# Expert matmuls of a hybrid encoder step: one 32-bit product for a high/low split, and six weight buffers for three

## The chip, the cores and the metric

One core of a Trainium2 chip. The metric is the device time of one execution in microseconds (us), the median of several runs. The kernel before takes 1567.64 us (three runs, 1567.49 to 1568.17).

## What is computed

One layer of a streaming encoder on 288 rows (256 prompt rows and 32 sample rows), width 2048, all in float32: a projection `h @ w_in` to 8704 columns, stick-breaking and sliding-window attention, two output projections merged under sigmoid gates, `w_out`, and then the part that the change touches, a mixture of 16 gated experts of which each row uses two:

```python
def hier_moe(h, ...):
    ...
    for e in range(N_EXPERTS):
        a = jax.nn.silu(hf @ w_e_gate[e]) * (hf @ w_e_up[e])
        y = y + gate[:, e:e + 1] * (a @ w_e_down[e])
```

`w_e_gate` and `w_e_up` are 16 x 2048 x 512, `w_e_down` is 16 x 512 x 2048: 12 MB of weights for each expert, 192 MB in all.

## The kernel before, in words

Everything up to the experts is not rewritten by the change: the projections work through `w_in`, `w_sb_o`, `w_swa_o` and `w_out` in blocks of 128 columns. ScalarE copies a block into `wh` (type F32R, L590), VectorE puts the rest into `wl` (L1206), and TensorE makes three products for each of 16 contraction tiles (`products`, L865 to L867). A queue of SyncE loads the blocks as pairs into `ring`; the last four iterations (IT_OUT to IT_END) load `w_out`. `load` then fetches the three matrices of expert 0 into `slot_g` (gate), `slot_d` (down) and `slot_u` (up), 4 MB each. GpSimd meanwhile brings `xT` back from memory for the residual sum.

Then `choose` (VectorE) compares row ranks with 0 to 63 and so makes `pick`, a matrix of 0 and 1 that picks the rows of one expert, 64 slots. `gather` (TensorE, L1064) multiplies `pick` with the rows `x2` (three bf16 parts, three row tiles: nine matmuls for each of 16 tiles of 128 columns, 144 in all) and so leaves the expert's rows, transposed, in banks 0 and 1. `slot_rms` (L1072) gathers the row scales, and `gathered` (L1479) multiplies by the norm's weight into `hg`, 128 x 16 x 64.

The expert's matmuls run in F32R. `hgx` holds beside each other the F32R copy of `hg` (64 columns, L767) and what it leaves out (64 columns, L1487). Each of 24 pieces of an expert's weights (128 x 1024) is copied by ScalarE into `eh` (`high`, L760), and VectorE, or GpSimd for pieces 1, 9 and 18, puts the rest into `el` (`low_part`, L340). TensorE makes two matmuls with `eh` and two with `el`, all with `hgx` as the stationary operand, whose 128 columns fill all 128 partitions of the result bank (`up_gate_piece`, L1090). Partitions 0 to 63 and 64 to 127 are then added up (L781, L1564 for the gate, L789, L1567 for up), ScalarE applies silu (L785), VectorE multiplies (L1570). Four matmuls turn the product (L1110), it is split again into `aTx` (L792, L1578), and pieces 16 to 23 multiply with it into banks 4 to 7 (L1120). ScalarE copies the upper halves into `y_sb` (L806), VectorE adds the lower ones (L1591), and SyncE writes the rows (L434).

The order of the work is written out by hand. TensorE's queue gathers the rows of the next expert one tile behind each piece from the fourth piece on, the last three tiles behind the sixteenth. SyncE waits until the last piece of a matrix is split (`low_wait`) and then loads the same matrix of the next expert (`next_matrices`).

```python
sem, w = piece(c)
act.wait_ge(S[sem], s * 16 + 16 * (1 + c // CH))
act.wait_ge(S["ch_used"], used(s, c - AHEAD - 1))
a_.activation(eh[c % 4][:], w, ACT.Copy).then_inc(S["eh_ready"], 1)
...
for low, part in enumerate((eh[c % 4], el[c % 4])):
    for k in range(2):
        kt = c % 8 * 2 + k
        mm = mm_(ps[2 + c // 8][:], hgx[:, kt, :], part[:, k * DE:(k + 1) * DE],
                 start=(low == 0 and kt == 0), stop=(low == 1 and kt == KT - 1))
```

Of the kernel before, what the change touches and what calls it, by code (L numbers as in the profile page):

```python
# [30 lines left out]
F32 = mybir.dt.float32  # L31
F32R = mybir.dt.float32r
# [7 lines left out]
P = 128  # L40
# [26 lines left out]
PIECE = D // 2  # L67
CH = 24
BY_POOL = (1, 9, 18)
AHEAD = 3  # L70
# [22 lines left out]
def constants():  # L93
# [27 lines left out]
    for t, n in enumerate(TILES):  # L121
# [6 lines left out]
RAISED = """z_sb o_sb h_turned pool_head m_done a_ready y_out nat_done zm_done e_done o_sb_ev nat_free  # L128
            rope_done ml_done y_act y_dve aT_ps aTl_done table_in ev_a ev_d""".split()
# [31 lines left out]
def build(nc, x_prompt, x_sample, cache_sb_k, cache_sb_v, cache_swa_k, cache_swa_v, w_in, b_gate, swa_sink,  # L161
# [66 lines left out]
    slot_g = at("slot_g", 100, [P, KT, DE])  # L228
    slot_u = at("slot_u", 132, [P, KT, DE])
    slot_d = at("slot_d", 0, [P, FT, D])  # L230

    places = (164, 168, 172, 176, 180, 184, 188, 60)
    eh = [at(f"eh{j}", places[2 * j], [P, PIECE], F32R) for j in range(AHEAD + 1)]
    el = [at(f"el{j}", places[2 * j + 1], [P, PIECE], F32R) for j in range(AHEAD + 1)]

# [4 lines left out]
    hgx = at("hgx", 32, [P, KT, 2 * SLOTS], F32R)  # L240
    hg = at("hg", 40, [P, KT, SLOTS])
    aTx = at("aTx", 44, [P, FT, 2 * SLOTS], F32R)
    pick = at("pick", 46, [P, 3, SLOTS], BF16)
    y_sb = at("y_sb", 50, [SLOTS, D])
    g_sb = at("g_sb", 58, [SLOTS, DE])
    u_sb = at("u_sb", 201, [SLOTS, DE])
# [12 lines left out]
    gfin = at("gfin", 156, [P, D])  # L259
# [41 lines left out]
    with ExitStack() as ctx:  # L301
# [7 lines left out]
                   g_in u_in d_in picked hg_ps hg_sb hgh_done hgl_done eh_ready el_ready elp_ready ch_used g_low g_sum  # L309
                   silu_done u_low u_sum a_ready aT_ps aTh_done aTl_done y_act y_dve y_out  # L310
                   zero_set zero_out rows_ready ints_ready gf_in y_in0 y_in1 y_in2 sum_done fin out_done
                   ex_in ex_out half_done ssq3 rko_done ident_done rp_done x2_back all_rows table_in""".split()
# [16 lines left out]
        def piece(c):  # L329

            m, q = c % CH // 8, c % 8
            if m == 2:
                return "d_in", slot_d[:, q // 2, q % 2 * PIECE:(q % 2 + 1) * PIECE]
            w = (slot_g, slot_u)[m]
            return ("g_in", "u_in")[m], w[:, 2 * q:2 * q + 2, :].rearrange("p k n -> p (k n)")

        def low_part(eng, s, c):

            eng.wait_ge(S["eh_ready"], s * CH + (c + 1))
            (nc.gpsimd if eng.engine == mybir.EngineType.Pool else nc.vector).tensor_tensor(  # L340
                el[c % 4][:], piece(c)[1], eh[c % 4][:].bitcast(F32), ALU.subtract)\
                .then_inc(S["elp_ready" if c % CH in BY_POOL else "el_ready"], 1)

        def used(s, c):


            return s * CH + (c + 2 + AHEAD)

# [21 lines left out]
        def _(sp):  # L370
# [28 lines left out]
            with sp.Fori(IT_OUT, IT_END) as it:  # L399
# [4 lines left out]
            def load(dst, w, e, sem):  # L404
                sp.dma_start(dst[:], w[0, ds(e, 1)].rearrange("a (k p) n -> p (a k) n", p=P)).then_inc(S[sem], 16)

            sp.wait_ge(S["blk"], upto(IT_OUT - 1, 3))
            load(slot_g, w_e_gate, 0, "g_in")  # L410
            sp.wait_ge(S["wl_ready"], upto(IT_END - 1, 3))
            load(slot_d, w_e_down, 0, "d_in")
            sp.wait_ge(S["x2_d"], 12)
            load(slot_u, w_e_up, 0, "u_in")

            def low_wait(s, c):


                assert not any(c - AHEAD <= p <= c for p in BY_POOL)
                sp.wait_ge(S["el_ready"], s * (CH - len(BY_POOL)) + (c + 1 - sum(p <= c for p in BY_POOL)))  # L420
# [1241 lines left out]
```

## Time and profile before

| | |
|---|---|
| median of three runs | 1567.64 us |
| the profiled execution: span from first to last instruction | 1563.4 us |
| median less the span | 4.2 us |
| mean granted TensorE clock | 0.914 of 2.4 GHz |
| PE busy, DVE busy, ACT busy, POOL busy | 87%, 63%, 54%, 12% |
| read and written | 319.51 MB, 20.71 MB |
| first expert matmul, last expert matmul | 826.0 us, 1513.8 us |

The profiled execution's own time is its span and what lies around it; of that the profile shows the span, and the median of the runs lies 4.2 us above it. PE is TensorE's matmuls, PEld its loads of the stationary operand, DVE VectorE, ACT ScalarE, POOL GpSimd, SPq the queue of SyncE. A matmul in plain float32 appears as two records, one in F32R as one.

### The profile page before, as it was taken

The page shows a single profiled execution, that of the slowest core. Times are in us where ns is not written, and L with a number is a line of the kernel's source. Part 1 is how long each engine was busy: PE and PEld are TensorE (multiplying, and loading weights), DVE is VectorE, ACT ScalarE, POOL GpSimd, SP SyncE. Part 2 cuts the span into 40 slices and gives each one's busy share as a digit, 9 for nine tenths or more (in the row PEclk, how much of TensorE's full clock was granted, in tenths as well). Part 3 has the DMA queues.
Part 4 walks back from the last instruction along what each step waited for, and adds up shares of the span by engine and source line. Part 5 has one row for each costly group of instructions (what it writes and reads, how often), then busy time and mean ns, then how long its engine had stood idle before and what let it go on. Part 6 is the DMA issues. An engine that isn't in the chain of part 4 may idle for free.

```text
span 1563.4 us, 24761 instructions
## 1 busy us (share of the span) xinstructions
PE 1365.0 (87%) x9452; PEld 1151.7 (74%) x9452; DVE 978.9 (63%) x1156; ACT 846.1 (54%) x993; POOL 184.6 (12%) x154
## 2 busy tenths in 40 slices
PE   5989999799999999999968888888898889888861
PEld 3889999698889999989946666666666566666630
DVE  3524446434445545444547887778877887888876
ACT  3423232355555454532446777667766777677741
POOL 2100100111100000000001111111111111111111
PEclk9899999899999999999978998889988898889985
DMA  7664444413334444464635887878877887877805
GB/s 234 227 225 163 173 161 162 169 55 107 107 108 161 162 161 161 161 222 161 244 133 216 309 299 291 302 281 311 313 274 302 335 305 287 307 285 294 320 15 208
DMA packets 184097, 340.48 MB, mean 218 GB/s; under 512 B 2944, under 2 KB 105456, under 8 KB 173184
## 3 DMA queue, kind: packets, MB, share of 16 engines
q1 hardware_dynamic: 179760, 319.30, 56.5%
q0 software_dynamic: 3904, 17.22, 3.2%
q10 hardware_dynamic: 400, 3.51, 0.6%
q8 instruction: 22, 0.36, 0.1%
q14 instruction: 11, 0.09, 0.0%
HBM read 319.51 MB, written 20.71 MB: 218 GB/s over the span
## 4 chain that ended last, share of the span: by engine, by line
PE 54%; issue 22%; DVE 12%; ACT 8%; DMA 4%; DVEq 1%; ACTq 0%; POOL 0%; POOLq 0%; SPq 0%
PE bank L1090 16%; PE bank L865 8%; PE bank L867 7%; PE bank L866 7%; PE bank L1120 5%; PE bank L1064 5%; ACT eh L760 3%; DVE el L340 2%; DVE y_sb L1591 2%; PE bank L1110 1%; DMA ring<-in_w_in 1%; DVE g_sb L1570 1%; ACT wh L590 1%; PE bank L843 1%; DVE wl L1206 1%
## 5 line engine op out<-in xcount | busy, mean ns | idle before, releaser
L1206 DVE TENSOR_TENSOR wl<-ring,wh 128x2048 fp32r<-128x2048 f32 x100 | 229.2, 2293 | 214.7 <-ACT wh L590 214.6
L865 PE MATMUL bank<-xh,wh 128*128 128x288 f32 x1088 | 331.3, 305 | 10.9 <-DVE xl L1214 5.9
L866 PE MATMUL bank<-xl,wh 128*128 128x288 f32 x1088 | 324.0, 298 | 0.0
L867 PE MATMUL bank<-xh,wl 128*128 128x288 f32 x1088 | 323.2, 297 | 0.0
L590 ACT ACTIVATE wh<-ring 128x2048 fp32r<-128x2048 f32 x100 | 190.9, 1909 | 145.8 <-PE bank L867 133.7
L1090 PE MATMUL bank<-eh,hgx 128*128 128x512 f32 x512 | 200.1, 474 | 62.6 <-DVE el L340 42.2
L865 PEld LDWEIGHTS bank<-xh,wh 128*128 128x128 f32 x1088 | 206.7, 190 | 15.7 <-issue 8.7
L867 PEld LDWEIGHTS bank<-xh,wl 128*128 128x128 f32 x1088 | 207.9, 191 | 0.0
L866 PEld LDWEIGHTS bank<-xl,wh 128*128 128x128 f32 x1088 | 207.6, 191 | 0.3
L340 DVE TENSOR_TENSOR el<-slot_u,eh 128x1024 fp32r<-128x1024 f32 x112 | 143.9, 1305 | 50.4 <-ACT eh L760 50.2
L760 ACT ACTIVATE eh<-slot_d 128x1024 fp32r<-128x1024 f32 x128 | 133.7, 1055 | 68.8 <-PE bank L1120 48.2
L1090 PE MATMUL bank<-el,hgx 128*128 128x512 f32 x512 | 169.1, 412 | 0.0
L760 ACT ACTIVATE eh<-slot_u 128x1024 fp32r<-128x1024 f32 x128 | 134.2, 1055 | 56.3 <-PE bank L1090 56.1
L340 DVE TENSOR_TENSOR el<-slot_g,eh 128x1024 fp32r<-128x1024 f32 x112 | 157.7, 1447 | 5.6 <-ACT eh L760 5.5
L1064 PEld LDWEIGHTS bank<-pick,x 128*128 128x128 bf16 (+1 forms) x2304 | 100.9, 100 | 80.2 <-issue 57.9
L340 DVE TENSOR_TENSOR el<-slot_d,eh 128x1024 fp32r<-128x1024 f32 x112 | 135.4, 1223 | 38.3 <-ACT eh L760 38.0
L1090 PEld LDWEIGHTS bank<-eh,hgx 128*128 128x128 f32 x512 | 81.8, 200 | 100.9 <-DVE el L340 62.7
L1064 PE MATMUL bank<-pick,x 128*128 128x64 bf16 (+1 forms) x2304 | 143.2, 201 | 4.0 <-DVE pick L1472 4.0
L760 ACT ACTIVATE eh<-slot_g 128x1024 fp32r<-128x1024 f32 x128 | 126.2, 1044 | 17.8 <-PE bank L1090 17.8
L1090 PEld LDWEIGHTS bank<-el,hgx 128*128 128x128 f32 x512 | 103.2, 202 | 25.9
L1120 PE MATMUL bank<-eh,aTx 128*128 128x512 f32 x256 | 104.5, 497 | 19.0 <-DVE aTx L1578 19.0
L1120 PE MATMUL bank<-el,aTx 128*128 128x512 f32 x256 | 96.3, 463 | 0.0
(303 smaller groups left out, 1936.2 us busy)
## 6 DMA issues: line engine op xcount, KB each, us to landing
ring<-in_w_in SPq DMA_DIRECT2D x34, 2048.0 KB, 8.1
slot_g<-in_w_e_gate SPq DMA_DIRECT2D x16, 4096.0 KB, 13.2
slot_d<-in_w_e_down SPq DMA_DIRECT2D x16, 4096.0 KB, 12.9
slot_u<-in_w_e_up SPq DMA_DIRECT2D x16, 4096.0 KB, 13.3
ring<-in_w_out SPq DMA_DIRECT2D x8, 2048.0 KB, 7.6
ring<-in_w_sb_o SPq DMA_DIRECT2D x8, 1024.0 KB, 5.0
ring<-in_w_swa_o SPq DMA_DIRECT2D x8, 1024.0 KB, 7.2
y_rows<-y_sb SPq DMA_DIRECT2D x16, 512.0 KB, 7.2
```

The costliest lines, as they stand in the source:

```text
L340: (nc.gpsimd if eng.engine == mybir.EngineType.Pool else nc.vector).tensor_tensor(el[c % 4][:], piece(c)[1], eh[c % 4][:].bitcast(F32), AL ...
L590: a_.activation(wh[:, j % 2], raw(j), ACT.Copy).then_inc(S["wh_ready"], 1)
L760: a_.activation(eh[c % 4][:], w, ACT.Copy).then_inc(S["eh_ready"], 1)
L843: mm = tr(ps[2 + k % 3][:, t * P:t * P + n], x_nat[0:n, t, k * P:(k + 1) * P], ident[0:n, 0:n])
L865: mm_(dst, wh[:, j % 2, k, :], hi[:, k, :], start=(k == k0), stop=False)
L866: mm_(dst, wh[:, j % 2, k, :], lo[:, k, :], start=False, stop=False)
L867: mm = mm_(dst, wl[:, j % 2, k, :], hi[:, k, :], start=False, stop=(k == k1 - 1))
L1064: mm_(ps[k // 8][:, (k % 8) * SLOTS:(k % 8 + 1) * SLOTS], x2[j][0:n, t, k * P:(k + 1) * P], pick[0:n, t, :], start=(t == 0 and j == 0), st ...
L1090: mm = mm_(ps[2 + c // 8][:], hgx[:, kt, :], part[:, k * DE:(k + 1) * DE], start=(low == 0 and kt == 0), stop=(low == 1 and kt == KT - 1))
L1120: mm = mm_(ps[4 + q0 + q][:], aTx[:, f, :], part[:, q * 512:(q + 1) * 512], start=(low == 0 and f == 0), stop=(low == 1 and f == FT - 1))
L1206: v.tensor_tensor(wl[:, j % 2], raw(j), wh[:, j % 2].bitcast(F32), ALU.subtract)\
L1591: v.tensor_tensor(y, y, ps[4 + q][0:SLOTS, :], ALU.add).then_inc(S["y_dve"], 1)
```

## The change

For the experts alone, the split is taken out: the weights as they are loaded, float32, are the moving operand, `hg` (float32, 64 columns) is the stationary one, and the result fills partitions 0 to 63 of a bank; gate and up take turns tile by tile in banks 2 and 3. The three slots of 32 KB per partition become six homes of 16 KB: homes 0 to 3 hold four tiles of gate and four of up each, homes 4 and 5 half of down each. An expert's matrices are laid out so that partition p holds rows 16p to 16p+15 of gate and up (4p to 4p+3 of down): a home's load reads runs of 8 KB (gate, up) and 16 KB (down), where the loads before read 2 KB and 8 KB. So that the rows fit, `gather` and the turn read their stationary operand with a step: every 16th column of `x2`, every fourth of `g_sb`. SyncE loads a home again as soon as its matmuls are through. The gathering for the next expert stands in two pieces behind all of gate and up.

```diff
+    home = [at(f"home{c}", kb, [P, 4096]) for c, kb in enumerate((100, 116, 138, 154, 0, 16))]
...
+        def gate_up(half, k):
+            return home[k // KPC][:, half * 2048 + k % KPC * DE:half * 2048 + (k % KPC + 1) * DE]
+        def down(f, q):
+            return home[GU + f // 2][:, f % 2 * D + q * 512:f % 2 * D + (q + 1) * 512]
...
+            def load_home(c, e):
+                if c < GU:
+                    for half, w in enumerate((w_e_gate, w_e_up)):
+                        src = w[0, ds(e, 1)].rearrange("a (p k) n -> p (a k) n", p=P)[:, c * KPC:(c + 1) * KPC, :]
+                        sp.dma_start(home[c][:, half * 2048:(half + 1) * 2048].rearrange("p (k n) -> p k n", n=DE), src)\
+                            .then_inc(S[f"home_in{c}"], 16)
+                else:
+                    f = 2 * (c - GU)
+                    src = w_e_down[0, ds(e, 1)].rearrange("a (p f) n -> p (a f) n", p=P)[:, f:f + 2, :]
+                    sp.dma_start(home[c][:].rearrange("p (f n) -> p f n", n=D), src).then_inc(S[f"home_in{c}"], 16)
...
             def next_matrices(e, s):
-                low_wait(s - 1, 7)
-                load(slot_g, w_e_gate, e, "g_in")
-                low_wait(s - 1, 15)
-                load(slot_u, w_e_up, e, "u_in")
-                low_wait(s - 1, 23)
-                load(slot_d, w_e_down, e, "d_in")
+                for c in range(HOMES):
+                    sp.wait_ge(S["ch_used"], s * HOMES + (c + 1 - HOMES))
+                    load_home(c, e)
...
+                act.wait_ge(S["ch_used"], s * HOMES + GU)
+                a_.activation(g_sb[:], ps[2][0:SLOTS, :], ACT.Silu, scale=stat[0:SLOTS, 24:25])\
+                    .then_inc(S["silu_done"], 1)
                 act.wait_ge(S["aT_ps"], s + 1)
+                a_.activation(aT[:], ps[4][:, 0:FT * SLOTS].rearrange("p (f n) -> p f n", f=FT), ACT.Copy)\
+                    .then_inc(S["aT_sb"], 1)
...
+                for k in range(k0, k1):
+                    for t, n in enumerate(TILES):
+                        for j in range(3):
+                            mm_(ps[k // 8][:, (k % 8) * SLOTS:(k % 8 + 1) * SLOTS],
+                                x2[j][0:n, t, k:D:KT], pick[0:n, t, :],
...
             def expert(s, nxt):
+                pe.wait_ge(S["hg_sb"], s * 2 + 2)
+                for k in range(KT):
+                    c = k // KPC
+                    if k % KPC == 0:
+                        pe.wait_ge(S[f"home_in{c}"], s * 32 + 32)
+                    for half in range(2):
+                        mm = mm_(ps[2 + half][0:SLOTS, :], hg[:, k, :], gate_up(half, k),
+                                 start=(k == 0), stop=(k == KT - 1))
+                    if k % KPC == KPC - 1:
+                        mm.then_inc(S["ch_used"], 1)
                 if nxt:
+                    gather(s + 1, 0, 12)
+                pe.wait_ge(S["a_ready"], s + 1)
                 for f in range(FT):
-                    mm = mm_(ps[2][:, f * SLOTS:(f + 1) * SLOTS], g_sb[:, f * P:(f + 1) * P],
+                    mm = mm_(ps[4][:, f * SLOTS:(f + 1) * SLOTS], g_sb[:, f:DE:FT],
                              ident[0:SLOTS, 0:SLOTS], start=True, stop=True)
                 mm.then_inc(S["aT_ps"], 1)
+                if nxt:
+                    gather(s + 1, 12, KT)
+                    pe.wait_ge(S["y_dve"], s + 1)
+                    slot_rms()
+                pe.wait_ge(S["aT_sb"], s + 1)
+                if nxt:
+                    pe.wait_ge(S["hg_sb"], s * 2 + 4)
...
+                for f in range(FT):
+                    if f % 2 == 0:
+                        pe.wait_ge(S[f"home_in{GU + f // 2}"], s * 16 + 16)
+                    for q in range(4):
+                        mm = mm_(ps[4 + q][0:SLOTS, :], aT[:, f, :], down(f, q),
+                                 start=(f == 0), stop=(f == FT - 1))
```

How the order moves on TensorE's queue, in the body of the loop over the experts. Before, a piece and the gathering behind it stand so (`eh_108` and `el_112` are the fourth buffers of the two parts, `x_0` to `x_2` the three bf16 parts of `x2`; a row is one instruction, or several of the same with x):

```order
L1082 REGISTER_ALU
L1090 MATMUL bank<-eh_108,hgx 128x512 [waits el_ready]
L1090 MATMUL bank<-eh_108,hgx 128x512
L1090 MATMUL bank<-el_112,hgx 128x512 x2
L1064 MATMUL bank<-pick,x_0_113 128x64
L1064 MATMUL bank<-pick,x_1_114 128x64
L1064 MATMUL bank<-pick,x_2_115 128x64
```

Each piece waits for its own `el`. In the changed kernel the loop begins with all of gate and up (`home_102` to `home_105` are homes 0 to 3), and the gathering stands behind it:

```order
+L1009 ISA [waits hg_sb]
+L1011 MATMUL bank<-home_102,hg 64x512 [waits home_in0]
+L1011 MATMUL bank<-home_102,hg 64x512 x7
+L1011 MATMUL bank<-home_103,hg 64x512 [waits home_in1]
+L1011 MATMUL bank<-home_103,hg 64x512 x7
+L1011 MATMUL bank<-home_104,hg 64x512 [waits home_in2]
+L1011 MATMUL bank<-home_104,hg 64x512 x7
+L1011 MATMUL bank<-home_105,hg 64x512 [waits home_in3]
+L1011 MATMUL bank<-home_105,hg 64x512 x7
+L987 ISA
+L991 MATMUL bank<-pick,x_0_108 128x64 [waits picked]
```

Thirty-two matmuls for gate and up stand where 64 stood, and none of them waits for another engine's work on the weights. The end of the same body, from the last rows of the gathering to the down matmuls:

```order
+L991 MATMUL bank<-pick,x_2_110 128x64
+L999 MATMUL bank<-rparts,pick 64x1 [waits y_dve]
+L999 MATMUL bank<-rparts,pick 64x1 x8
+L1028 REGISTER_ALU [waits aT_sb]
+L1033 ISA [waits y_dve,y_act,hg_sb]
+L1035 MATMUL bank<-home_106,aT 64x512 [waits home_in4]
+L1035 MATMUL bank<-home_106,aT 64x512 x7
+L1035 MATMUL bank<-home_107,aT 64x512 [waits home_in5]
+L1035 MATMUL bank<-home_107,aT 64x512 x7
```

Sixteen matmuls stand for 32, and ahead of them a wait that was not there: for `hg_sb`, the rows of the next expert. On SyncE's queue, homes 0 and 1 of expert 0 now stand between two pairs of `w_out`:

```order
+L356 DMA ring<-in_w_out 128x16x256 [waits wl_ready] x2
+L384 DMA home_102<-in_w_e_gate 128x2048 [waits blk]
+L384 DMA home_102<-in_w_e_up 128x2048
+L384 DMA home_103<-in_w_e_gate 128x2048
+L384 DMA home_103<-in_w_e_up 128x2048
```

Before, the first expert load stood behind all of the `w_out` loads.

## Rows read from the trace of the kernel before

**Rows 1.** The page, chain that ended last: shares of the span by engine

```profile
PE 54%; issue 22%; DVE 12%; ACT 8%; DMA 4%; DVEq 1%; ACTq 0%; POOL 0%; POOLq 0%; SPq 0%
```

**Rows 2.** Stretch, its us, busy PE, PEld, DVE, ACT, POOL; clock, DMA share, GB/s

```profile
826.00:1472.50 646.50, 570.38 (x3856) 404.40 (x3856) 523.75 (x536) 459.11 (x520) 111.43 (x45) 0.88 0.80 297
```

**Rows 3.** Waits of PE in the expert stage: us in total, times, longest

```profile
PE bank L1090 <- DVE el L340: 42.2, 16, 2.8
PE bank L1120 <- DVE aTx L1578: 19.0, 16, 2.4
```

**Rows 4.** Timeline of PE, one expert: start us, us, what, count, idle before

```profile
1013.53 0.54 PE L1064 MATMUL bank<-pick,x 128*128 128x64 bf16 x9
1013.99 0.73 PE L1090 MATMUL bank<-eh,hgx 128*128 128x512 f32 x2
1014.57 0.63 PE L1090 MATMUL bank<-el,hgx 128*128 128x512 f32 x2
1015.03 0.54 PE L1064 MATMUL bank<-pick,x 128*128 128x64 bf16 x9
...
1024.07 1.95 PE L1064 MATMUL bank<-pick,x 128*128 128x64 bf16 x36
1025.95 0.53 PE L1072 MATMUL bank<-rparts,pick 128*64 128x1 bf16 x9
1026.85 1.81 PE L1110 MATMUL bank<-con,g_sb 64*128 64x64 f32 x8 [0.37 <-DVE g_sb L1570]
1029.77 1.22 PE L1120 MATMUL bank<-eh,aTx 128*128 128x512 f32 x2 [1.10 <-DVE aTx L1578]
1030.78 1.05 PE L1120 MATMUL bank<-el,aTx 128*128 128x512 f32 x2
```

**Rows 5.** Timeline of PE, the plain float32 logits (288 columns moving)

```profile
787.90 5.03 PE L1021 MATMUL bank<-xT,wr 128*20 128x288 f32 x20
792.86 1.53 PE L1016 MATMUL bank<-con,xT 128*128 128x128 f32 x12
```

**Rows 6.** Timeline of PE, a plain float32 matmul of 448 columns in attention

```profile
322.30 0.91 PE L966 MATMUL bank<-spb,con 128*128 128x448 f32 x2
323.05 0.38 PE L967 MATMUL bank<-spb,con 128*128 128x128 f32 x2
```

**Rows 7.** Timeline of all engines, from the first gathering to the first expert matmul

```profile
810.33 11.25 PE L1064 MATMUL bank<-pick,x 128*128 128x64 bf16 x144 [3.95 <-DVE pick L1472]
...
821.50 0.73 PE L1072 MATMUL bank<-rparts,pick 128*64 128x1 bf16 x9
822.27 1.29 DVE L1479 TENSOR_TENSOR hg<-bank,par 128x512 f32<-128x512 f32 x2 [11.41 <-PE bank L1072]
...
826.04 1.22 PE L1090 MATMUL bank<-eh,hgx 128*128 128x512 f32 x2 [3.81 <-DVE hgx L1487]
```

**Rows 8.** Timeline of PE, first and last matmuls of the last expert

```profile
1472.49 0.70 PE L1090 MATMUL bank<-eh,hgx 128*128 128x512 f32 x2
...
1513.15 0.63 PE L1120 MATMUL bank<-el,aTx 128*128 128x512 f32 x2
```

**Rows 9.** The chain that ended last, behind the last expert

```profile
1517.64 4.31 DMA y_rows<-y_sb
```

**Rows 10.** Timeline of DVE at the first residual sums of w_out

```profile
688.26 0.45 DVE L1364 TENSOR_TENSOR xT<-xT,bank 128x288 f32 x1 [8.07 <-DMA xT<-xT_spill]
```

**Rows 11.** DMA issues of the page: KB each, us to landing

```profile
slot_g<-in_w_e_gate SPq DMA_DIRECT2D x16, 4096.0 KB, 13.2
```

**Rows 12.** Two stretches of PE: its us, busy us; clock, DMA share, GB/s

```profile
815.00:820.00 5.00, 5.00 (x67) 0.50 0.01 3
1024.10:1026.90 2.80, 2.43 (x47) 1.00 0.99 364
```

**Rows 13.** Groups of PEld: loads of the stationary operand, busy us and mean ns

```profile
L1090 PEld LDWEIGHTS bank<-eh,hgx 128*128 128x128 f32 x512 | 81.8, 200 | 100.9 <-DVE el L340 62.7 <-POOL el L340 23.4 <-issue 4.3
L1064 PEld LDWEIGHTS bank<-pick,x 128*128 128x128 bf16 x1536 | 64.1, 103 | 65.6 <-issue 57.9 <-DVE rk L1467 4.0
```

More of the change, by code:

```diff
@@ L66 @@
 PAIR = 2 * P
[L67 to L70, printed above, removed]
+HOMES = 6
+GU = 4
+KPC = KT // GU
 FAR = 1000.0
@@ L239, in build @@
     lgT = at("lgT", 58, [NL, NT])
-    hgx = at("hgx", 32, [P, KT, 2 * SLOTS], F32R)
-    hg = at("hg", 40, [P, KT, SLOTS])
-    aTx = at("aTx", 44, [P, FT, 2 * SLOTS], F32R)
+    hg = at("hg", 32, [P, KT, SLOTS])
+    aT = at("aT", 36, [P, FT, SLOTS])
+    y_sb = at("y_sb", 38, [SLOTS, D])
+    g_sb = at("g_sb", 58, [SLOTS, DE])
+    gf_pk = at("gf_pk", 205.90625, [P, KT])
     pick = at("pick", 46, [P, 3, SLOTS], BF16)
-    y_sb = at("y_sb", 50, [SLOTS, D])
-    g_sb = at("g_sb", 58, [SLOTS, DE])
-    u_sb = at("u_sb", 201, [SLOTS, DE])
     su_b = at("su_b", 206, [P, P], BF16)
@@ L398, in _ @@
                         .then_inc(S["w_load1"], 16)
-            with sp.Fori(IT_OUT, IT_END) as it:
+            def load_home(c, e):
[8 more added lines that the diff above has]
+                    sp.dma_start(home[c][:].rearrange("p (f n) -> p f n", n=D), src).then_inc(S[f"home_in{c}"], 16)
+            for j in range(2):
+                slot_free(j, IT_OUT)
+                load_pair(j, w_out[0, :, j * PAIR:(j + 1) * PAIR])
+            sp.wait_ge(S["blk"], upto(IT_OUT - 1, 3))
+            load_home(0, 0)
+            load_home(1, 0)
+            with sp.Fori(IT_OUT + 1, IT_END) as it:
                 for j in range(2):
@@ L815, in _ @@
+            with act.Fori(0, NE) as e:
+                expert(e)
             act.wait_ge(S["ints_ready"], 1)
@@ L818, in _ @@
                 with act.Fori(0, more) as i:
-                    tokens_high(i + NE)
-                    for c in range(AHEAD):
-                        high(i + NE, c)
-                    expert(i + NE, False)
+                    expert(i + NE)
             for t, n in enumerate(TILES):
@@ L1124, in _ @@
             pe.wait_ge(S["rk_done"], 1)
-            for k in range(KT):
-                gather(0, k)
+            gather(0, 0, KT)
             pe.wait_ge(S["rp_done"], 1)
@@ L1135, in _ @@
                 with pe.Fori(0, more) as i:
-                    for k in range(KT):
-                        gather(i + NE, k)
-                    pe.wait_ge(S["aTl_done"], i + (NE + 1))
+                    gather(i + NE, 0, KT)
                     slot_rms()
@@ L1453, in _ @@
             v.tensor_copy(MMb[:], MM).then_inc(S["masks"], 1)
-            def lows(s, *cs):
-                for c in cs:
-                    if c % CH not in BY_POOL:
-                        low_part(dve, s, c)
-            lows(0, 0)
             dve.wait_ge(S["masks"], 1)
```

211 lines of the change are left out of this document (36 added, 175 removed).

## Prediction

> **What bounds the kernel now.** The chain of waits comes first: TensorE holds 54% of it and "issue" 22%, VectorE and ScalarE 20% together, DMA 4% [rows 1]. The table of stretches says where the change can act: from 826 to 1472.5 us stand fifteen experts, 43.1 us each, with TensorE's matmuls busy 570 of 646.5 us, VectorE 524, ScalarE 459, and the DMA engines 80% at 297 GB/s [rows 2]. The waits in this stage are small: 42.2 us for `el`, 19.0 us for `aTx`, over all sixteen experts [rows 3], some 4 us of the 43 for each. So the stage is TensorE's stream with small holes, and what the change does to that stream decides. The question for the timeline is then what one matmul of each kind costs from start to start. In the steady part of an expert the pair with `el` starts at 1014.57 and its successor at 1015.03: 0.23 us for a matmul of 512 columns; nine gathering matmuls take 0.46 us, 52 ns each [rows 4]. Gate and up are 64 such matmuls, down 32: 22 us of the period. Gathering is 7.5 us.
>
> **The price of a plain float32 matmul** is not in the expert stage, but it is in the trace. The logits move 288 columns of float32 in two records each: 20 records, ten matmuls, from 787.90 to 792.86, so 0.248 us a record, 0.496 us a matmul [rows 5]. In attention one matmul of 448 columns starts at 322.30 and what follows it at 323.05: 0.75 us [rows 6]. Both give 1.67 to 1.72 ns a column; the logits have only 20 stationary columns and the other 128, so the count of stationary columns does not set it, and the 64 of `hg` lie between. For 512 columns I take the longer one's rate, which is the nearer in size: 512 x 0.75 / 448 = 0.857 us (by the logits' rate 0.88). That is 3.7 times an F32R matmul of as many columns, and the change halves their number only: 32 + 16 matmuls, 41.1 us, for 96 that take 22.1.
>
> **The sum, part by part, for one expert at full clock.** (1) Gate and up: 32 x 0.857 = 27.4 us. No `eh` or `el` to wait for; the holes of 4 us go. (2) Gathering, twelve tiles: 108 x 0.052 = 5.6 us. It stands in its own stretch now; before it stood between the pieces, and cost TensorE the same. It covers silu and the product, two operations on 64 partitions, after which the turn can start. (3) The turn: 8 records. At the lower clock they take 1.8 us [rows 4]; I take 1.3. (4) Four more tiles, 1.9 us as in [rows 4], which cover the copy into `aT`. (5) `slot_rms`, then the new wait. Behind the gathering of expert 0, `slot_rms` starts at 821.50, the two products into `hg` at 822.27 and take 1.29 us [rows 7]; with a small copy ahead of them TensorE could go on at 823.8. From that 2.3 us at half clock; 2.1 us here. Queued behind this wait are all down matmuls, and nothing else is there for TensorE. (6) Down: 16 x 0.857 = 13.7 us. (7) The clock. Behind the gathering, `slot_rms` and the small waits of [rows 4] the granted clock falls to 1.2 GHz: the pair at 1029.77 lasts 1.22 us and the next 1.05, where full-clock pairs last 0.63 to 0.73. The new order has the same low stretch ahead of down; some 4 us of down at half clock lose 2.0 us. Sum: 54.0 us, against 43.1.
>
> The last expert has no gathering: 27.4 + about 1.6 for silu and product + 1.6 + 0.6 for turn and copy + 13.7 + 2.0 = 46.9 us. It took 41.3 us, from 1472.49 to 1513.8 [rows 8].
>
> **What lies around it.** The split of the tokens into `hgx` goes, so the first expert starts at 823.8 instead of 826.04 [rows 7]; but the clock is still at its lower level there, and 5 us at the doubled price cost 2.6. Fifteen periods and the last: 823.8 + 2.6 + 15 x 54.0 + 46.9 = 1683.3 us, 169.5 later than 1513.8. Behind it, four copies and four sums of `y_sb` become two copies on each of two engines: rows went out 3.8 us after the last matmul [rows 8, 9], now about 1.5, so -2.3. Homes 0 and 1 are loaded between the `w_out` pairs, while `xT` is still on its way; VectorE waits 8.07 us for it already, until 688.26 [rows 10]. 4 MB take 13.2 us [rows 11]. The bounds are 0 and, if `xT` shares the engines all the way, 4; I take 2. The next pair has some 8 us of slack, so it still comes in time. GpSimd's three pieces and all of `eh` and `el` go at nothing: with the holes of (1) counted, no one waits for them. The sum is 169.2: 1563.4 becomes 1732.6, and with the 4.2 by which the median lies above the span, **1737 us**.
>
> **DMA.** It would have to bring three times 4 MB in a period, 39.6 us at 13.2 us each [rows 11], and there are 54. Homes 0 to 3 come free every 6.9 us of gate and up, the last two in and behind down; each is needed 40 us later. Longer runs only make this looser. It is no bound, and faster loads give nothing.
>
> **The largest unknown** is the step in the gathering's stationary operand, every 16th column of bf16. No row of the trace has such a load. The lower bound is the contiguous load, no extra cost. A gathering matmul takes 52 ns at full clock, and 11.17 us / 144 = 77.6 at half [rows 7, 12]: the 64 moving columns are 27 and 53 ns, so 25 ns are the load's and do not follow the clock. A float32 load of 128 columns lasts 200 ns and the bf16 one 103 [rows 13]; as an upper bound a step could make a bf16 load as slow as that, some 85 to 97 ns more. Between them I take the lower end, as the row of the same operation and size with only the step changed is the nearest. The Trainium skill's page "SBUF — State Buffer" (section "Door 1: The DMA port swizzle") speaks against it: consecutive accesses have full bandwidth within a line of 16 bytes, and each crossing to a new line pays a penalty; here every column crosses. By it the sum would be that of the first rival, and no run here shows it yet.
>
> **Rivals.** *The stepped load costs once more what the contiguous one does*: 77 ns at full clock, 103 at half. TensorE streams less of the time, so the clock falls inside the first gathering run, as it never rises when gathering runs alone [rows 12]. 43 matmuls at 77 ns, 65 at 103: 10.1 us for 5.6, then 3.7 for 1.9, and 0.6 in the small steps; 6.9 a period, 15 times, and 3.7 for expert 0: **1844 us**. The Trainium skill's page named above argues for it. *It costs as much as a float32 load*: 137 and 162 ns, 15.6 a period and 11.8 at the start: 1983. *A float32 matmul into 64 partitions costs half of what the rows say* (the other side): then expert matmuls take 20.6 us, a period some 34 and the loads bound it at 39.6 and rows going out, 41: about **1530 us**. It decides below 0.63 us a matmul, where the period would be 43.1 again. The records at 20 and at 128 stationary columns speak against it, two for each matmul [rows 5, 6]. *Loads come late after all*, since each home waits for its own release and is split in two issues: 5 us a period, 1815. *The clock doesn't rise under float32 at 64 columns*: 82 us of matmuls, about 2350; in [rows 5] it stayed at full through 5 us of such matmuls (0.248 us for 2 x 288 columns is the 2.4 GHz level).
>
> **How the numbers follow.** Forecast 0.53; the doubled load 0.22; as slow as float32 0.10; late loads 0.05; clock 0.02; half the price 0.04; 0.04 for what I don't see, which falls near no change for 0.01. The forecast's own range is 1705 to 1765: 0.02 us on the matmul (0.88 for 0.857) is 1.1 a period and 17 in all, the clock 0 to 4 us a period's half-rate loss, and 2 for `xT`. To hold eight in ten the range must take in the doubled load: 1700 to 1865. Left out are the slow end and the fast one. A measurement of this kernel can tell 0.2%, 3 us, from no change. Faster by more than that 0.04, within it 0.01, slower 0.95.
>
> **What would show it.** Right, if PE's records in the experts start 0.43 us apart at full clock, two a matmul; if the period is 54 us; if home waits are absent from TensorE's waits; and if gathering matmuls stand 52 ns apart. If they stand 77 ns or more apart, the rival with the stepped load holds. If the record count is one a matmul, or the distance is half, the price was wrong and the kernel may be faster. A large wait for a DMA on TensorE would break the paragraph on DMA.

## The result, and the profile after

| | before | the change |
|---|---|---|
| median (range) | 1567.57 us (4 runs) | 1850.47 us (1848.20 to 1851.52, 4 runs) |
| ratio to before, with its 95% interval | 1 | 1.180 (1.1784 to 1.1817) |
| span of the profiled execution | 1563.4 us | 1846.5 us |
| mean granted TensorE clock | 0.914 | 0.902 |
| one expert, start to start | 43.1 us | 61.5 us |

The kernel is 18% slower. The direction was forecast, the size not: 1850 stands 113 us above the 1737 of the forecast and 6 us above the 1844 of the first rival, the stepped load. It is outside the forecast's own range (1705 to 1765) and inside the wide one (1700 to 1865), which had been stretched to take in that rival. The chain that ended last in the profile after answers to [rows 1]; then its costliest groups on TensorE, by line, engine, operands, count, busy us and mean ns:

```profile
PE 84%; DVE 5%; ACT 4%; DMA 3%; issue 3%; ACTq 0%; POOL 0%; DVEq 0%; POOLq 0%; SPq 0%
...
L1011 PE MATMUL bank<-home,hg 128*64 128x512 f32 x1024 | 444.0, 594 | 1.5 <-DVE hg L1387 1.5
...
L1035 PE MATMUL bank<-home,aT 128*64 128x512 f32 x512 | 264.5, 682 | 23.2 <-DVE hg L1387 22.7
```

The records are two a product, as forecast: 512 products of gate and up are 1024 records. VectorE and ScalarE, 20% of the chain in [rows 1], are 9% of it now. That is visible in the stretch of fifteen experts too, whose columns are those of [rows 2]:

```profile
827.70:1750.50 922.80, 900.07 (x3855) 416.79 (x3856) 56.32 (x132) 30.98 (x58) 0.00 (x0) 0.86 0.56 210
```

VectorE fell from 524 us busy to 56 and ScalarE from 459 to 31, the DMA engines from 80% to 56%, and TensorE rose from 570 us to 900. Nearly all that the change took away was work of engines that stood beside the path. What that work had cost TensorE is its idle time, 76 us of the 646.5 in [rows 2]; now it is 23 of 922.8, so some 3.5 us a period were won. The timeline of PE for one expert, beside [rows 4], says what the 61.5 us are (start, us, what, count, idle before):

```profile
1197.61 27.63 PE L1011 MATMUL bank<-home,hg 128*64 128x512 f32 x64
1225.17 9.87 PE L991 MATMUL bank<-pick,x 128*128 128x64 bf16 x108
1234.97 2.12 PE L1019 MATMUL bank<-con,g_sb 64*128 64x64 f32 x8
1237.03 3.43 PE L991 MATMUL bank<-pick,x 128*128 128x64 bf16 x36
1240.38 0.72 PE L999 MATMUL bank<-rparts,pick 128*64 128x1 bf16 x9
1242.62 16.59 PE L1035 MATMUL bank<-home,aT 128*64 128x512 f32 x32 [1.51 <-DVE hg L1387]
```

Gate and up start 27.56 us ahead of the first gathering: 0.861 us a product. The gatherings are what stands out, 9.80 us for 108 (forecast 5.6). Four stretches of this expert, in the columns of [rows 2], show the clock in the first and second part of the first gathering run and of down:

```profile
1225.20:1230.20 5.00, 5.00 (x59) 4.52 (x59) 0.74 (x1) 0.68 (x1) 0.00 (x0) 1.00 0.74 279
1230.90:1234.90 4.00, 4.00 (x45) 3.44 (x45) 0.00 (x0) 0.00 (x0) 0.00 (x0) 0.50 0.23 96
1242.70:1247.30 4.60, 4.60 (x6) 1.36 (x7) 0.00 (x0) 0.00 (x0) 0.00 (x0) 0.50 0.00 0
1247.70:1258.90 11.20, 11.20 (x27) 3.66 (x26) 0.00 (x0) 0.00 (x0) 0.00 (x0) 0.99 0.49 187
```

The clock falls to 1.2 GHz inside the gatherings and stays there for the first 5 us of down. From start to start in the trace a gathering takes 89 ns at full clock and 93 at half, so its price hardly follows the clock. The groups of PEld that answer to [rows 13]:

```profile
L991 PEld LDWEIGHTS bank<-pick,x 128*128 128x128 bf16 x1536 | 116.8, 162 | 27.1 <-issue 12.2 <-DVE rk L1374 1.7
...
L1019 PEld LDWEIGHTS bank<-con,g_sb 64*128 64x128 f32 x128 | 31.0, 324 | 3.3 <-DVE g_sb L1459 2.4
```

The load of the same 128 x 128 bf16 values lasts 162 ns where it lasted 103. TensorE's waits in the expert stage, instead of those of [rows 3], hold no DMA:

```profile
PE bank L1035 <- DVE hg L1387: 22.7, 15, 1.5
PE bank L1019 <- DVE g_sb L1459: 1.6, 1, 1.6
```

### The profile page after: what moved, and what is told of

The parts are those of the page before. It is cut to its first block, busy times and chain, and to the rows that moved or that the text cites. A ratio compares the mean times of both kernels' runs of the same rounds, so it can differ in the third digit from the quotient of the medians.

```text
span 1846.5 us, 22766 instructions
## 1 busy us (share of the span) xinstructions
PE 1716.6 (93%) x9452; PEld 1166.2 (63%) x9452; DVE 475.5 (26%) x724; ACT 389.6 (21%) x500; POOL 62.8 (3%) x107
## 4 chain that ended last, share of the span: by engine, by line
PE 84%; DVE 5%; ACT 4%; DMA 3%; issue 3%; ACTq 0%; POOL 0%; DVEq 0%; POOLq 0%; SPq 0%
PE bank L1011 24%; PE bank L1035 14%; PE bank L991 11%; PE bank L796 10%; PE bank L798 10%; PE bank L797 10%; PE bank L1019 2%; ACT wh L567 1%; DVE hg L1387 1%; DMA ring<-in_w_in 1%; DVE wl L1119 1%; PE bank L774 1%; DMA xT<-xT_spill 1%; DMA yb<-y_rows,rows 1%; DMA con<-in_const 1%
## 5 line engine op out<-in xcount | busy, mean ns | idle before, releaser
L1011 PE MATMUL bank<-home,hg 128*64 128x512 f32 x1024 | 444.0, 594 | 1.5 <-DVE hg L1387 1.5
L1011 PEld LDWEIGHTS bank<-home,hg 128*64 128x64 f32 x1024 | 140.7, 137 | 301.6 <-issue 301.6
L1035 PE MATMUL bank<-home,aT 128*64 128x512 f32 x512 | 264.5, 682 | 23.2 <-DVE hg L1387 22.7
L991 PE MATMUL bank<-pick,x 128*128 128x64 bf16 (+1 forms) x2304 | 213.0, 244 | 1.6 <-DVE pick L1379 1.6
L991 PEld LDWEIGHTS bank<-pick,x 128*128 128x128 bf16 (+1 forms) x2304 | 183.8, 158 | 40.9 <-issue 12.2
L1035 PEld LDWEIGHTS bank<-home,aT 128*64 128x64 f32 x512 | 78.9, 158 | 196.2 <-issue 195.5
L796 PE MATMUL bank<-mh,wh 128*128 128x288 f32 x256 | 77.5, 303 | 6.5 <-DVE wl L1119 3.5
L796 PE MATMUL bank<-oh,wh 128*128 128x288 f32 x256 | 75.9, 297 | 1.8 <-DVE wl L1119 1.8
L797 PE MATMUL bank<-ml,wh 128*128 128x288 f32 x256 | 76.8, 300 | 0.0
L798 PE MATMUL bank<-mh,wl 128*128 128x288 f32 x256 | 76.5, 299 | 0.0
```

The source lines that it names most:

```text
L796: mm_(dst, wh[:, j % 2, k, :], hi[:, k, :], start=(k == k0), stop=False)
L797: mm_(dst, wh[:, j % 2, k, :], lo[:, k, :], start=False, stop=False)
L798: mm = mm_(dst, wl[:, j % 2, k, :], hi[:, k, :], start=False, stop=(k == k1 - 1))
L991: mm_(ps[k // 8][:, (k % 8) * SLOTS:(k % 8 + 1) * SLOTS], x2[j][0:n, t, k:D:KT], pick[0:n, t, :], start=(t == 0 and j == 0), stop=(t == 2 ...
L1011: mm = mm_(ps[2 + half][0:SLOTS, :], hg[:, k, :], gate_up(half, k), start=(k == 0), stop=(k == KT - 1))
L1035: mm = mm_(ps[4 + q][0:SLOTS, :], aT[:, f, :], down(f, q), start=(f == 0), stop=(f == FT - 1))
```

## The experiments

"Period" is the time from the first gate product of expert 0 to that of the last, over fifteen, in the profiled execution. All ratios are to the kernel before, measured beside the run. Averages of a part of an expert are from the start of the part to the start of the next, over fifteen experts.

### Is it the step? Short runs again, nothing stepped

```diff
-    src = w[0, ds(e, 1)].rearrange("a (p k) n -> p (a k) n", p=P)[:, c * KPC:(c + 1) * KPC, :]
+    src = w[0, ds(e, 1)].rearrange("a (k p) n -> p (a k) n", p=P)[:, c * KPC:(c + 1) * KPC, :]
...
-    x2[j][0:n, t, k:D:KT], pick[0:n, t, :],
+    x2[j][0:n, t, k * P:(k + 1) * P], pick[0:n, t, :],
...
-    g_sb[:, f:DE:FT]
+    g_sb[:, f * P:(f + 1) * P]
```

Down's load and the norm weights of `hg` follow.

> The step alone undone, with the runs it bought: feature k*128+p on partition p again for gate and up, feature f*128+p for down, so the gatherings and the turn load adjacent columns and the weights arrive in runs of 2 KB and 8 KB. Unsplit 32-bit products, six homes and their order stay. Theory 1 (the 61.5 us of an expert are 48 full products at 0.858 us, plus 40 ns more for each of 144 gatherings because their stationary operand is stepped by 32 bytes, plus a clock that falls in them): a gathering goes back to 52 ns at full clock (78 at half), the first expert product starts up to 5.9 us earlier (13.4 us to 7.5, or 11.2 at half clock), and a period falls to between 55 and 59 us: 1740 to 1810 us in all, against 1850 with the step. Theory 2 (a gathering is slow because the engine has just done 32-bit work, or because of the clock): it stays near 92 ns and the time within 10 us of 1850. Theory 3 (the long runs carry the transfers): the transfers of an expert grow past 55 us, PE waits for the homes, and the time is above 1850.

Measured: 1755.47 us, ratio 1.117 (1.111 to 1.123), period (1663.78 - 824.81) / 15 = 55.9 us. One expert on PE, then the load's group:

```profile
1162.53 27.63 PE L1011 MATMUL bank<-home,hg 128*64 128x512 f32 x64
1190.09 5.96 PE L991 MATMUL bank<-pick,x 128*128 128x64 bf16 x108
1195.98 1.97 PE L1019 MATMUL bank<-con,g_sb 64*128 64x64 f32 x8
1197.88 2.87 PE L991 MATMUL bank<-pick,x 128*128 128x64 bf16 x36
1200.68 0.72 PE L999 MATMUL bank<-rparts,pick 128*64 128x1 bf16 x9
1202.91 16.87 PE L1035 MATMUL bank<-home,aT 128*64 128x512 f32 x32 [1.51 <-DVE hg L1387]
```

```profile
L991 PEld LDWEIGHTS bank<-pick,x 128*128 128x128 bf16 x1536 | 66.3, 104 | 28.9 <-issue 12.2 <-DVE rk L1374 1.7
```

The gathering is back at 52 ns at full clock and its load at 104. The spans differ by 89 us: 84 are 5.6 us in each of fifteen periods, 2.9 the earlier start of expert 0. No wait for a home appears with runs of 2 KB. Theories 2 and 3 fall. But the clock still falls, and down still takes 16 us.

Where it falls now differs from one expert to the next, with the same instructions. The expert shown is a long one, 57.1 us at a mean clock of 0.88; four of the fifteen take 54.3 to 54.5 at 0.94, and in them the clock stays at full through the turn, which then takes 1.03 us instead of 1.90. The four executions of this kernel spread likewise, from 1739 to 1759 us. In the change the clock fell inside the first gathering run in every one of the fifteen, and the periods behind the first agree within 0.2 us.

### The same with the long runs kept

```diff
-    a_.activation(x2[0][0:n, t, q * 512:(q + 1) * 512], x2_bank(q, t)[0:n], ACT.Copy)
+    a_.activation(packed(x2[0][0:n, t, :], q), strided(x2_bank(q, t)[0:n]), ACT.Copy)
```

`strided` views 512 features as 16 by 32, `packed` puts feature p*16+k at column k*128+p; all pieces, `g_sb` and the residual sum are viewed likewise.

> Long runs kept, both steps undone in another way: the token values are stored so that the columns of one gathering lie side by side (the pieces are written and the residual added back through reordered views), and the gated product is written in the turn's order. Theory 1 (step alone): same period as with short runs, 55 to 59 us; the reordered writes of the token values cost 0 to 10 us once before the experts; 1745 to 1820 us. Theory 2: near 1850. Theory 3 (runs matter): this one is faster than the one with short runs by more than the 10 us of the reordering; under theory 1 it is not.

Measured: 1765.49 us, ratio 1.127 (1.124 to 1.131); period (1664.98 - 824.51) / 15 = 56.0. The same period as with short runs: the long runs bring nothing where TensorE is the bound. The 10 us more are the most that the forecast gave the reordering. The profiled executions are 4 us apart, 1.5 of it in the periods and 2.9 behind the last expert's start, where VectorE adds the residual through reordered views (12 sums, 13.0 us for 8.9).

### How the price grows with the step

```diff
-    x2[j][0:n, t, k:D:KT], pick[0:n, t, :],
+    x2[j][0:n, t, k % 3:k % 3 + STEP[k] * (P - 1) + 1:STEP[k]], pick[0:n, t, :],
```

> The 16 groups of nine gatherings read their 128 columns at steps of 1, 1, 1, 2, 2, 2, 4, 4, 4, 8, 8, 8, 16, 16, 1, 1 columns of 2 bytes: the gathered values are those of wrong columns, and what follows from them too. If the price goes by lines of 16 bytes, steps of 1 take 52 ns at full clock, 2, 4 and 8 grow with the bytes that one column spans, and 16 is no dearer than 8 (92 ns). If any step pays the whole price, 2 already takes 92 ns. If the cost is not the step's, all take 92 ns.

Measured: 1794.96 us in one run, of which only the trace counts here. Stretches of the first gathering run at steps 1, 2, 4 and 8, cut a little inside each, in the columns of [rows 2] with PE alone:

```profile
1205.45:1206.80 1.35, 1.35 (x27) 1.00 0.22 36
1206.90:1208.25 1.35, 1.35 (x28) 1.00 0.80 279
1208.40:1209.90 1.50, 1.50 (x28) 1.00 1.00 421
1210.00:1212.20 2.20, 2.20 (x27) 0.70 0.95 402
```

From start to start in the trace, meaned over fifteen experts: 52.4 ns at step 1, 52.6 at step 2 (4 bytes), 59.2 at step 4 (8 bytes), 87.6 at step 8 (16 bytes) before the clock falls; in the change, at step 16 (32 bytes) and full clock, it is 88.8. At half clock expert 0 gives 78, 78, 80, 94, and 94 at step 16. So the price is reached once each column has 16 bytes to itself, and more step costs hardly more. That is the pattern of the 16-byte line of the Trainium skill's page "SBUF — State Buffer" (section "Door 1: The DMA port swizzle"), which asks for at least two accesses in a line for full bandwidth; at step 4, which has two, the rows show a loss of 7 ns and not none.

### Two halves of the array

```diff
-    mm = mm_(ps[2 + half][0:SLOTS, :], hg[:, k, :], gate_up(half, k),
+    mm = mm_(ps[2 + half][half * SLOTS:(half + 1) * SLOTS, :], hg[:, k, :], gate_up(half, k),
...
-    mm = mm_(ps[4 + q][0:SLOTS, :], aT[:, f, :], down(f, q),
+    mm = mm_(ps[4 + q][q % 2 * SLOTS:(q % 2 + 1) * SLOTS, :], aT[:, f, :], down(f, q),
```

The readers of these banks follow.

> The change as it is, except that the up product goes to partitions 64 to 127 of its bank while gate stays at 0 to 63, and of down's four products the second and fourth go to 64 to 127. Theory A (the two column halves of the array work at the same time): a pair of 32-bit products takes about the 0.858 us of one, 24 of 48 products cost nothing, and PE's work in a period falls from 61.5 by 20.6 us to 41; the 8 MB of an expert, 39.6 us at the rate of the kernel before, come close behind: 1540 to 1580 us. Theory B (single file whatever the halves): within 5 us of 1850.

Measured: 1521.01 us, ratio 0.971 (0.968 to 0.974), period 41.0. The start of one expert's gate and up, in the change and here, 2.31 us of each (the last number is the count):

```profile
1197.61 2.31 PE L1011 MATMUL bank<-home,hg 128*64 128x512 f32 x5
```

```profile
1197.23 2.31 PE L1011 MATMUL bank<-home,hg 128*64 128x512 f32 x10
```

and the loads of the second kernel:

```profile
1197.24 0.14 PEld L1011 LDWEIGHTS bank<-home,hg 128*64 128x64 f32 x2 [0.29 <-issue]
1197.67 0.14 PEld L1011 LDWEIGHTS bank<-home,hg 128*64 128x64 f32 x2 [0.29 <-issue]
```

Ten records in the time of five: the two of a pair start some 5 ns apart and the next pair 0.43 us later. Theory A holds: 13.8 us for gate and up instead of 27.6, and the kernel is faster than the one before although every gathering is still stepped. The time lies 19 us below the range that was given it, which had room for loads that come close behind; the period is the 41 us of PE's work and no wait for a home shows. The Trainium skill's page "TensorEngine Tiling (Array Packing)" (section "Key Properties") says that different tiles can load and multiply in parallel; the trace agrees for plain float32.

### Two halves without the step, with long and with short runs

> Two halves (gate to partitions 0 to 63, up to 64 to 127, down's products likewise) and both steps undone with the long runs kept. PE alone: 41.0 us of a period, less the 5.5 that undoing the step took off the single file (61.5 to 56.0): 35.5 us. Theory 1 (PE still ends last): 35.5 us for an expert, 1521 less 15 times 5.5 and less 2 at the start, about 1435. Theory 2 (the transfers end last): 12.6 MB and the rows come no faster than in 39.6 us, the period is then near 40 and the time near 1505; waits for homes show on PE.

> The same with the short runs (2 KB for gate and up, 8 KB for down) and nothing of the token values reordered. If the run length sets the rate of the transfers and these end last, it is slower than the one with long runs by more than 10 us; if the transfers don't bind, or run length does not set their rate, it is the faster of the two by up to 10 us (the reordered writes are gone), near 1430.

These join the edits shown above. Measured: long 1423.03 us, ratio 0.908 (0.906 to 0.910); short 1416.98 us, 0.904 (0.901 to 0.906). Both periods are 34.8 us. Theory 1 holds, with times 12 and 13 us below the forecasts: 12.6 MB of weights came in 34.8 us and no wait for a home shows, so 39.6 us, which the forecast had from slots that were loaded whole, was no limit. The short runs are ahead by 6 us in the median, with executions that overlap (1412 to 1422 and 1421 to 1427). In the profiled ones, 4.7 us apart, expert 0 starts 2.7 us earlier and 1.7 lie behind the experts' last start, where the reordered views are read. That the reordering causes the 2.7 is not shown: in the pair of kernels without halves above the start is 0.3 us later with short runs.

### Gatherings spread between the gate and up products

```diff
     if k % KPC == KPC - 1:
         mm.then_inc(S["ch_used"], 1)
+    if nxt and k >= 8:
+        gather(s + 1, k - 8, k - 7)
 if nxt:
-    gather(s + 1, 0, 12)
+    gather(s + 1, 8, 12)
```

> The change as it is, except that 8 of the 16 groups of nine gatherings follow the eight last steps of gate and up one by one, and 4 are left ahead of the turn. Theory 1 (the clock falls because all gatherings stand in one stretch, and costs 2.7 us in down and 0.5 in the turn): the clock stays up longer, a period falls from 61.5 by 1 to 3 us, 1805 to 1835 in all. Rival (each change between the two kinds of product costs PE a drain, 16 changes more in a period; or the clock falls as deep, only elsewhere): the period stays or grows, 1850 or more.

> Two halves, short runs, no step, and the gatherings spread as in the run before it. If the clock is what spreading gives back, it is 15 to 40 us below the one that is not spread; if the transfers end last by then, the same as that one; if changing between full-width and half-width products costs a drain each time, it is slower.

Measured: 1850.63 us, ratio 1.181 (1.179 to 1.184), period 61.6: nothing gained. With two halves 1427.82 us, 0.912 (0.910 to 0.913), 11 us slower than unspread. The first:

```profile
1162.72 1.93 PE L1011 MATMUL bank<-home,hg 128*64 128x512 f32 x4
1164.59 0.86 PE L991 MATMUL bank<-pick,x 128*128 128x64 bf16 x9
1165.38 1.93 PE L1011 MATMUL bank<-home,hg 128*64 128x512 f32 x4
...
1176.53 2.13 PE L1021 MATMUL bank<-con,g_sb 64*128 64x64 f32 x8
...
1184.18 15.78 PE L1037 MATMUL bank<-home,aT 128*64 128x512 f32 x32 [1.52 <-DVE hg L1389]
```

From the start of one gathering group to the next there are 2.66 us, where four records (1.72) and nine gatherings (0.80) make 2.52: 0.14 us a round trip, 1.1 us in eight. Down falls from 16.4 to 15.6, 0.8 back, and the clock had fallen all the same by the turn, whose 2.06 us are those of the lower clock. A cost and a gain of nearly the same size cancel here.

With two halves and no step a round costs about the same 0.14 us, and down takes 9.0 us on average with and without the spreading. But the clock does behave otherwise. In all fifteen experts it is still at full in the turn, and falls in the gatherings behind it or just after them:

```profile
1163.58 1.10 PE L1021 MATMUL bank<-con,g_sb 64*128 64x64 f32 x8
1164.62 2.72 PE L991 MATMUL bank<-pick,x 128*128 128x64 bf16 x36
```

The turn gains 0.4 us a period by that (1.03 for 1.42), less than the eight rounds cost: the period is 35.25 us for 34.79. The Trainium skill's page "TensorEngine Tiling (Array Packing)" (section "Key Properties") names a drain at a change of tiling. The 0.14 us fit it, but no run here shows what the cost consists of.

### The start: first homes later

```diff
-            sp.wait_ge(S["blk"], upto(IT_OUT - 1, 3))
-            load_home(0, 0)
-            load_home(1, 0)
             with sp.Fori(IT_OUT + 1, IT_END) as it:
...
+            sp.wait_ge(S["blk"], upto(IT_OUT - 1, 3))
+            load_home(0, 0)
+            load_home(1, 0)
```

> The change as it is, except that homes 0 and 1 of expert 0 are loaded behind all of w_out's pieces instead of between the first two pieces and the others. Theory (the read-back of xT, 13.6 us instead of 10.9, shares the DMA engines with these 4 MB; DVE and with it PE wait 2.7 us longer, and the clock is at half from 691.6 to 698.4, which costs PE 4 more): the first expert product starts about 5 us earlier, 822 to 824 in place of 827.7, and the total is about 1845. Rival (the wait is of something else, or the clock falls in any case): the start stays within 1 us.

Measured: 1844.71 us, ratio 1.1779 (1.1752 to 1.1805), against 1850.47 and 1.180. The two ratios are not clear of each other, since the kernel before was 3 us faster too beside this run; the case rests on the start of expert 0 in the traces. First a stretch of the change, then the same of this kernel, in the columns of [rows 2]; before, it looked like the second, clock 1.00:

```profile
691.80:698.20 6.40, 5.95 (x25) 5.95 (x26) 2.97 (x3) 0.00 (x0) 0.00 (x0) 0.50 0.87 300
```

```profile
691.80:698.20 6.40, 6.40 (x50) 6.40 (x50) 2.15 (x2) 1.62 (x1) 0.00 (x0) 1.00 0.55 171
```

In the same 6.4 us TensorE has 25 products in the one and 50 in the other. VectorE's wait for `xT` [rows 10], in the change and then here:

```profile
689.54 0.45 DVE L1277 TENSOR_TENSOR xT<-xT,bank 128x288 f32 x1 [10.76 <-DMA xT<-xT_spill]
```

```profile
687.08 0.45 DVE L1277 TENSOR_TENSOR xT<-xT,bank 128x288 f32 x1 [7.83 <-DMA xT<-xT_spill]
```

TensorE waits behind it for VectorE's `wl` (waits between 660 and 826 us), in the change and then here:

```profile
PE bank L796 <- DVE wl L1119: 3.5, 1, 3.5
```

```profile
PE bank L796 <- DVE wl L1119: 0.6, 1, 0.6
```

Expert 0 starts at 822.4 instead of 827.7. The collision of the loads costs 2 to 3 us of waiting and, through the 6.8 us at half clock that begin in the longer wait, as much again.

### The wait before down

```diff
-    mm = mm_(ps[7][0:SLOTS, 0:1], pick[0:n, t, :], rparts[0:n, j, t:t + 1],
+    mm = mm_(ps[2][0:SLOTS, 0:1], pick[0:n, t, :], rparts[0:n, j, t:t + 1],
...
-    if nxt:
-        pe.wait_ge(S["hg_sb"], s * 2 + 4)
```

> The change as it is, except that the scales of the gathered rows go to bank 2 (free since the gated product) instead of bank 7, so that down no longer waits until DVE has read them. Theory (step 5's 1.5 us of waiting stand on PE's path in each period): a period falls from 61.5 to 60.0, the total by 22 us to about 1828. Rival (the next gate and up wait for the same tokens, or the clock makes up the idle time): unchanged, 1845 to 1850.

Measured: 1819.58 us, ratio 1.162 (1.160 to 1.165), period (1725.86 - 827.65) / 15 = 59.9. The period falls by 1.6 us, 24.7 in fifteen, which is also the difference of the spans: the wait stood on the path whole. (The medians are 31 us apart, because the execution profiled here was the slowest of its four and that of the change the fastest.)

### All of it, and how near the transfers are

> Two halves, short runs without step, homes 0 and 1 later, no wait before down. If each gives what it gave or should give alone: 1417 less 5 for the start less 15 times 1.5 for the wait, 1390. If the transfers end last below 34.8 us a period (12.6 MB and 0.5 MB of rows in 33.3 us are 390 GB/s), PE waits for homes instead and it stays near 1417.

Measured: 1408.51 us, ratio 0.899 (0.896 to 0.901), the fastest kernel of the study. The period is (1333.40 - 822.68) / 15 = 34.05 us, 0.7 less than with the wait where 1.5 was expected; it isn't the transfers, since no wait for a home shows. One expert:

```profile
1196.71 13.90 PE L1011 MATMUL bank<-home,hg 128*64 128x512 f32 x64
1210.54 5.71 PE L991 MATMUL bank<-pick,x 128*128 128x64 bf16 x108
1216.18 1.74 PE L1019 MATMUL bank<-con,g_sb 64*128 64x64 f32 x8
1217.86 2.87 PE L991 MATMUL bank<-pick,x 128*128 128x64 bf16 x36
1220.66 0.72 PE L999 MATMUL bank<-rparts,pick 128*64 128x1 bf16 x9
1221.31 9.74 PE L1032 MATMUL bank<-home,aT 128*64 128x512 f32 x32
```

The lower clock has taken back what is missing. Down averages 9.4 us for 9.0 with the wait, 5.1 of them at half clock for 4.3; the turn averages 1.65 for 1.42 and the gatherings behind it 2.7 for 2.4. One expert of the fifteen shows what the clock alone is worth. It is the first of these two stretches, each nearly a whole expert, in the columns of [rows 2]; the second is the expert shown above:

```profile
995.70:1027.00 31.30, 31.30 (x259) 14.25 (x257) 3.95 (x9) 2.25 (x4) 0.00 (x0) 0.95 1.03 405
1196.80:1230.80 34.00, 34.00 (x259) 15.93 (x257) 3.95 (x9) 2.25 (x4) 0.00 (x0) 0.85 1.00 384
```

The same 259 records take 2.7 us less at a clock of 0.95 than at 0.85. Order and waits are those of its neighbours, so the order of the instructions alone does not decide where the clock falls.

Then gate and up at half width:

```diff
-    mm = mm_(ps[2 + half][half * SLOTS:(half + 1) * SLOTS, :], hg[:, k, :], gate_up(half, k),
+    mm = mm_(ps[2 + half][half * SLOTS:(half + 1) * SLOTS, 0:DE // 2], hg[:, k, :], gate_up(half, k)[:, 0:DE // 2],
```

> The kernel of the last run with gate and up computed for the first 256 of their 512 columns only (the other 256 columns of both are left as they stand in the banks, so the experts' results are those of half the product); all transfers stay. It shows how near the transfers are to being the bound. PE alone: gate and up fall from 14.0 to 7.0 us, a period from 34.05 to 27.1. Theory 1 (the kernel before set the rate: 39.6 us for an expert): already refuted, since 34.05 us periods were seen without a wait. Theory 2 (the transfers can run at the 434 GB/s that single stretches showed): 13.1 MB take 30.2 us, PE waits for homes and the period is 30 to 31, some 1350 in all. Theory 3 (there is more to be had): the period falls to 27.

Measured: 1357.36 us, period (1288.26 - 822.45) / 15 = 31.05. PE's waits, and the stretch of fifteen experts in the columns of [rows 2]:

```profile
PE bank L1011 <- DMA home<-in_w_e_up: 35.9, 16, 3.2
```

```profile
822.40:1288.20 465.80, 429.82 (x3855) 247.69 (x3857) 57.83 (x133) 32.54 (x58) 0.00 (x0) 0.79 1.02 410
```

Here the transfers end last, at 410 GB/s over the stage. Single periods range from 26.7 to 37.6 us, so it is their mean that the transfers set. The fastest kernel stands 3 us a period above this floor.

## Why the prediction was right and wrong

**The price of a float32 product: right.** 0.857 us was forecast, 0.861 measured over gate and up, two records each, 0.43 us apart. (1) took 27.7 us for 27.4. This alone makes the change lose: 48 x 0.86 us against 22 us for the split products of [rows 4]. With the step undone the kernel was still 12% slower than before. What the six homes do with the split kept, no run here shows.

**The stepped operand: the term that failed.** The forecast set it to nothing, "as the row of the same operation and size with only the step changed is the nearest". That row had the operation and lacked the one property in question; the operand's layout was the difference. (2) took 9.8 us for 5.6 and (4) 3.4 for 1.9. Undoing the step gave back 5.6 of the 7.5 us by which the period missed: 4.1 in (2), 0.8 in (4), 0.5 in the turn, 0.3 in down. The rival had 77 ns at full clock and 103 at half; measured are 89 and 93. Its two errors cancel, 13.8 us for 144 gatherings against 13.2, and so its total of 1844 is nearly exact by luck. Its form was not: it had the price rise by 26 ns from full to half clock, and the rows show 4. What it had right and the forecast wrong is that the step costs, and that the clock falls inside the first gathering run. The forecast says that by the 16-byte line of the Trainium skill's page the sum would be the rival's; the page says that a crossing pays a penalty and gives no size for it. The 25 ns of the rival came from rows.

**The clock: (3), (4), (6) and (7).** The low stretch was forecast ahead of down only. It starts in the first gathering run, so the turn and the last four tiles run in it too, which (3) and (4) had at or near full clock. (3) took 2.06 us for 1.3: without the step the turn takes 1.03 us at full clock and 1.90 at half, so most of its miss is the clock, and the step, whose float32 columns stand 16 bytes apart, adds 0.16. (4) takes 1.9 us at full clock and 2.8 at half without the step, 3.4 with it. (6) and (7) took 16.4 us together for 15.7, of which 5.3 were at half clock for the 4 of the forecast. Without the step the clock falls in the same region, but in some experts only behind the turn.

**The wait (5)** took 2.24 us for 2.1 and stands on the path, as said.

Summed: 0.3 + 4.2 + 0.8 + 1.5 + 0.1 + 0.7 = 7.6 us a period, 113 us in fifteen, the whole of the miss. The rest cancels. Unstepped, the forecast's 54.0 us meet 55.9: without the step it would have been 18 us low, half of it in (3) and (4) by the clock, and just inside its own range. By its own signs the forecast fails on two (a period of 54 us, gatherings 52 ns apart) and holds on two (records 0.43 us apart, no wait for a home).

**The start.** Expert 0 began at 827.7; the forecast had 823.8 and 2 us more for `xT`. The stepped gatherings are 13.4 us for 11.2. The collision with `xT` was given 2 us and costs 5 to 6: the wait was seen, the clock behind it not. That the miss is not larger is owed to a gain that nobody forecast. With the collision gone the gatherings start at 806.8 where they started at 810.3 before; 2.3 us of that are TensorE's wait for `pick`, 1.6 us now for the 3.95 of [rows 7]. **DMA no bound** was right; its figure of 39.6 us was no measure of what the transfers can do. The rival on the other side, products at half the price, did not occur in the change. In the kernel with two halves two products share the time of one, and the time came out near that rival's 1530; but the rival had its period of 41 us from the loads, and there it was TensorE's.

## What to carry to other kernels

Where products leave half of the array's columns idle, try sending them alternately to both halves of the partitions: with 64 stationary columns in plain float32 that halved their cost here, and alone turned an 18% loss into a 3% gain, and with the step, a wait and a collision of loads gone into 10%. The split products fill all 128 columns, and nothing of this applies to them. Ask of a new layout who else reads the tensor: longer runs in memory were bought with a stationary operand whose columns stand 16 bytes or more apart, which cost 5.6 us an expert where the runs gave nothing. And an operand's step belongs to the likeness of rows: a row with another step is no nearest row.

## What the runs showed of the hardware

- A bf16 stationary operand of 128 columns costs 52 ns a product of 64 columns at steps of 2 and 4 bytes, 59 at 8 bytes, 88 to 89 at 16 and 32 bytes; at half clock it is 78 at the small steps and 93 to 94 at 16 and 32 bytes.
- Two float32 products into partitions 0 to 63 and 64 to 127 of different banks start 5 ns apart and take together what one takes.
- A round between full-width gatherings and half-width products costs 0.14 us.
- The transfers of this stage ran at 410 GB/s over 466 us, with runs of 2 and 8 KB.
- With a wait of TensorE that was 2.9 us longer (3.5 for 0.6) came 6.8 us at half clock, from the wait on, in which it got through half as many products.
- One kernel ran an expert in 31.4 us at a mean clock of 0.95 and another in 34.2 at 0.85, with the same instructions and no wait in either.
- What exactly makes the clock fall in and behind the gatherings was not settled. With two halves and the gatherings spread it stayed at full through the turn in every one of fifteen experts, and fell in the gatherings behind it or just after them. Taking a 1.5 us wait away ahead of down left down as it was without halves (16.3 and 16.4 us) and went with a slower down in two halves (9.4 and 9.0, where the first loads were moved too). No order that was tried keeps the clock up all through.
